# Transpositions, value products and score products issued one by one between the projection matmuls of a two-layer attention trunk, and another order of a layer's first weight splits

## The reference

```python
h = rms_norm(x, norm1_g)
(a_q, a_k, a_v, b_q, b_k, b_v, c_qkv, d_cq, d_ckv, d_kr, gates) = split(h @ w_in)
oa = windowed_gqa(a_q, a_k, a_v, ...)           # 8 heads, band of 128
ob = differential_attention(b_q, b_k, b_v, ...) # 4 heads x 2 maps, full
oc = dilated_attention(c_qkv, ...)              # 3 patterns x 8 heads, softmax over patterns
od = latent_attention(d_cq, d_ckv, d_kr, ...)   # 8 heads, full, two low-rank projections
merged = sum(sigmoid(gate_i) * (o_i @ w_branch[i]) for i, o_i in enumerate((oa, ob, oc, od)))
x = x + merged @ w_o
u = depthwise_conv(rms_norm(x, norm2_g) @ ffn_w_up, ...)
x = x + (silu(g) * up) @ ffn_w_down             # g, up = split(u)
```

## Time and profile before

| | |
|---|---|
| three runs, median (lowest to highest) | 3001.43 us (2998.47 to 3010.02) |
| the profiled execution's own time | 3004.72 us |
| its span, first to last instruction | 3002.9 us |
| PE busy / weight loads busy | 2820.7 / 2267.0 us |
| DVE / ACT busy | 1566.0 / 1179.0 us |
| mean granted TensorE clock | 0.978 of 2.4 GHz |
| matmuls (and as many weight loads) | 13358 |

### The profile page before, as it was taken

One profiled execution on the slowest core, in us unless ns is written; L12 is line 12 of the kernel. 1 busy time (PEld: TensorE's weight loads), 2 busy tenths in 40 slices (PEclk: granted clock), 3 DMA queues, 4 the chain that ended last, 5 costly groups with the idle time before them and its releaser, 6 DMA issues.

```text
span 3002.9 us, 44753 instructions
## 1 busy us (share of the span) xinstructions
PE 2820.7 (94%) x13358; PEld 2267.0 (75%) x13358; DVE 1566.0 (52%) x3238; ACT 1179.0 (39%) x2387; POOL 0.6 (0%) x5
## 2 busy tenths in 40 slices
PE   5999989989989998999979999898899899999998
PEld 4889978666667887888868898776666678788887
DVE  5454476444445445555644544764354454465655
ACT  4444444434433234332434444534444332342432
POOL 0000000000000000000000000000000000000000
PEclk9999999889999999999989999999999999999999
DMA  4212222001112332333332122220111123223332
GB/s 152 72 48 72 78 63 85 12 29 41 45 37 78 94 96 78 99 98 99 99 100 64 44 78 79 67 85 1 36 43 50 31 91 98 92 85 98 95 96 91
DMA packets 141819, 217.62 MB, mean 72 GB/s; under 512 B 14777, under 2 KB 69387, under 8 KB 141195
## 3 DMA queue, kind: packets, MB, share of 16 engines
q1 hardware_dynamic: 132521, 200.62, 21.4%
q10 hardware_dynamic: 9058, 14.06, 1.4%
HBM read 206.20 MB, written 8.45 MB: 71 GB/s over the span
## 4 chain that ended last, share of the span: by engine, by line
PE 81%; DVE 9%; ACT 4%; issue 4%; ACTq 1%; DMA 1%; DVEq 0%; SPq 0%
PE bank L452 21%; PE bank L454 20%; PE bank L453 20%; PE bank L665 7%; PE bank L655 6%; PE bank L503 5%; DVE s_work L1563 1%; DVE s_wl L1139 1%; ACT s_wh L776 1%; ACT s_work L1027 1%; DVE s_work L1294 1%; PE bank L539 1%; ACTq L874 1%; DMA s_raw<-in_w_in 0%; ACT s_work L1019 0%
## 5 line engine op out<-in xcount | busy, mean ns | idle before, releaser
L1139 DVE TENSOR_TENSOR s_wl<-s_raw,s_wh 128x1024 fp32r<-128x1024 f32 (+2 forms) x372 | 453.6, 1220 | 526.5 <-ACT s_wh L776 525.9
L776 ACT ACTIVATE s_wh<-s_raw 128x1024 fp32r<-128x1024 f32 (+2 forms) x372 | 392.2, 1055 | 625.1 <-PE bank L454 591.9
L452 PE MATMUL bank<-s_hTh,s_wh 128*128 128x512 f32 x1216 | 486.2, 400 | 4.5 <-DVE s_work L1231 4.5
L454 PE MATMUL bank<-s_hTh,s_wl 128*128 128x512 f32 x1216 | 476.9, 392 | 0.0
L453 PE MATMUL bank<-s_hTl,s_wh 128*128 128x512 f32 x1216 | 476.7, 392 | 0.0
L452 PE MATMUL bank<-s_wh,s_hTh 128*128 128x512 f32 (+1 forms) x1088 | 475.8, 437 | 0.0
L454 PE MATMUL bank<-s_wh,s_hTl 128*128 128x512 f32 (+1 forms) x1088 | 427.0, 392 | 0.0
L453 PE MATMUL bank<-s_wl,s_hTh 128*128 128x512 f32 (+1 forms) x1088 | 426.7, 392 | 0.0
L1019 ACT ACTIVATE s_work<-s_work,s_stat 128x128 f32<-128x128 f32 (+3 forms) x384 | 214.1, 558 | 369.5 <-DVE s_stat L1588 123.0
L1563 DVE COPY s_work<-bank 128x256 f32<-128x256 f32 (+1 forms) x288 | 105.2, 365 | 394.5 <-ACT s_work L1027 391.9
L503 PE MATMUL bank<-s_consts,s_work 128*128 128x128 f32 (+1 forms) x1560 | 250.0, 281 | 47.3 <-DVE s_gTl L1495 14.3
(11 more groups left out here) (166 smaller groups left out, 3199.6 us busy)
## 6 DMA issues: line engine op xcount, KB each, us to landing
s_raw<-in_w_in SPq DMA_DIRECT2D x168, 512.0 KB, 3.4
s_raw<-in_ffn_w_up SPq DMA_DIRECT2D x176, 256.0 KB, 2.9
s_raw<-in_ffn_w_down SPq DMA_DIRECT2D x44, 512.0 KB, 3.7
s_raw<-in_w_branch SPq DMA_DIRECT2D x32, 512.0 KB, 3.6
s_raw<-in_w_o SPq DMA_DIRECT2D x16, 512.0 KB, 3.6
x_keep<-s_work ACTq DMA_DIRECT2D x2, 2048.0 KB, 7.5
s_raw<-in_w_in SPq DMA_DIRECT2D x16, 256.0 KB, 2.9
s_work<-x_keep ACTq DMA_DIRECT2D x2, 2048.0 KB, 8.2
```

The costliest lines, as they stand in the source:

```text
L452: mm(out, stationary[0], moving[0], start=start, stop=False)
L454: return mm(out, stationary[1], moving[0], start=False, stop=stop)
L776: a(wh[:, k % 3, 0:n], raw[:, s, 0:n], ACT.Copy).then_inc(*hi_split.up(own))
L1139: v.tensor_tensor(wl[:, k % 3, 0:n], raw[:, k % 2, 0:n], wh[:, k % 3, 0:n].bitcast(F32), ALU.subtract).then_inc(*tile_split.up(own))
```

## The change

A piece is now issued in parts. `transposed` yields between any two transpositions, `block` after every single dense matmul (1/6 of a step), and the values yield between any two key pieces. In a unit the transposition now comes right behind the scores (0.1 of the slot, then every 0.1), the values at 0.5 (then every 0.06), and the transposition of an output tile at 0.75 of step 10, 18, ... and no longer at the start of step 11, 19, .... The copies move with them. B's window reaches to four steps before gate1a, which doubles its length, and the norm of B's output follows it. Scores are still issued whole, between two single dense matmuls.

At the start of a layer ScalarE splits tiles 0 and 1 before it squares, and tile 2 after the second chunk of `norm_out`. VectorE splits tile 0 before the norm, tile 1 behind its parameter copy, and tile 2 after the second chunk.

```diff
-    ... B=(START["gate3a"] + 1, START["gate0a"], 32),
+    ... B=(START["gate3a"] + 1, START["gate1a"] - 4, 32),
...
                         for c in range(chunks):
-                            st, mv = operands(b, chunks * i + c, [t[:, c, :] for t in w])
-                            last = split3(PJ[b][:, 0:width], st, mv, i == 0 and c == 0, i == ntiles - 1 and c == chunks - 1)
+                            for st, mv in split3(*operands(b, chunks * i + c, [t[:, c, :] for t in w])):
+                                if n:
+                                    yield START[name] + 4 * i + b + n / (3 * chunks)
+                                n += 1
+                                last = mm(PJ[b][:, 0:width], st, mv, start=i == 0 and n == 1, stop=i == ntiles - 1 and n == 3 * chunks)
...
-            def transposed(dst, sources, at=0):
+            def transposed(dst, sources, done, when, pace, at=0):
 
-                for n, src in enumerate(sources, at):
+                for n, src in enumerate(sources):
+                    if n:
+                        yield when + n * pace
                     k, m = src.shape[0], src.shape[1]
-                    last = nc.tensor.transpose(dst[0:m, n * P:n * P + k], src, ident[0:k, 0:k])
-                return last
+                    last = nc.tensor.transpose(dst[0:m, (at + n) * P:(at + n) * P + k], src, ident[0:k, 0:k])
+                last.then_inc(*done.up())
...
+                yield from transposed(TD, sources, td_ready, when, 1 / 6)
...
+                        yield from transposed(TA, [probs[:, u % 2, P * k:P * k + P] for k in range(lo, hi)], ta_ready,
+                                              at + 0.1 * pace, 0.1 * pace, at=lo)
+                    if 2 <= step < n + 2:
+                        yield at + 0.5 * pace
...
+                        for k, (out, st, mv, start, stop) in enumerate(values_of(u, O1, probsT[:, u % 2, :])):
+                            if k:
+                                yield at + (0.5 + 0.06 * k) * pace
+                            last = mm(out, st, mv, start=start, stop=stop)
...
-            normalise()
-            for _k in range(3):
-                split_next()
+            split_next()
+            normalise()
...
             v.tensor_copy(prm[:, NROW + 88:NROW + 176], src[:, 256:344]).then_inc(*td_dve.up(own))
+            split_next()
...
-            norm_out(ROW["norm1"])
+            norm_out(ROW["norm1"], split_next)
```

More of the change, by code:

```diff
@@ L586, in dense, with turn @@
                     hidden += 2 * size
-            def turn(sources, *ready):
+            def turn(when, sources, *ready):
+                yield when
                 for handle, count in ready:
@@ L603, in head_turns @@
                     for t in range(4):
-                        yield begin + pace * t
                         n += 1
-                        turn(sources_of(t), normed.at(l, n))
+                        yield from turn(begin + pace * t, sources_of(t), normed.at(l, n))
                 def chunks_of(src):
@@ L629, in turns @@
                 for t in range(4):
-                    yield START["gate0a"] + 10 + 1.25 * t
-                    turn([oB[:, t, P * c:P * c + P] for c in range(4)], sublayer_normed.at(l, t + 1))
+                    yield from turn(B_NORM + 9 + 1.25 * t, [oB[:, t, P * c:P * c + P] for c in range(4)], sublayer_normed.at(l, t + 1))
             def attention(name, scores_of, values_of, per_out, begun, keys=all_keys, tile_of=None):
@@ L639, in attention @@
                 for step, at, pace in slots(name):
-                    if tile_of and step >= 11 and (step - 11) % 8 == 0:
-                        yield at
-                        tile = (step - 11) // 8
-                        pe.wait_ge(*o_out.at(l, outs + tile + 1))
-                        pe.wait_ge(*ta_act.at(l, n_att[0]))
-                        pe.wait_ge(*ta_dve.at(l, n_att[0]))
-                        n_att[0] += 1
-                        transposed(TA, tile_of(tile)).then_inc(*ta_ready.up())
                     if step < n:
@@ L656, in attention @@
                         last.then_inc(*s_ready.up())
[L657 to L666 removed]
                     if 1 <= step < n + 1:
[L668 removed]
+                        yield at + 0.1 * pace
                         u = step - 1
@@ L730, in _ @@
             pe.wait_ge(*params_in.at(l, 0))
-            turn([rows[:, n, :] for n in range(3)])
+            together(turn(0, [rows[:, n, :] for n in range(3)]))
             together(dense(), turns(), attentions())
@@ L1003, in attention @@
                 for step, at, pace in slots(name):
-                    if tile_at is not None and step >= 11 and (step - 11) % 8 == 0:
-                        yield at + 0.02 * pace
-                        t = (step - 11) // 8
-                        hi_out(gTh[:, tile_at:tile_at + 4, P * t:P * t + P], att_group(), ta_act)
                     if step < n:
@@ L1027, in attention @@
                         a(probsT[:, u % 2, P * lo:P * mid], src[:, P * lo:P * mid], ACT.Copy).then_inc(*ta_act.up(own))
+                    if tile_at is not None and step >= 10 and (step - 10) % 8 == 0:
+                        yield at + 0.82 * pace
+                        t = (step - 10) // 8
+                        hi_out(gTh[:, tile_at:tile_at + 4, P * t:P * t + P], att_group(), ta_act)
             def attentions():
@@ L1214, in normalise, with norm_out @@
                     v.tensor_scalar(h_sb[:, t, :], x_sb[:, t, :], stat[:, 2, t:t + 1], None, ALU.mult).then_inc(*h_normed.up(own))
-            def norm_out(row):
+            def norm_out(row, after_two=lambda: None):
                 for c in range(DC):
+                    if c == 2:
+                        after_two()
                     n_norm[0] += 1
@@ L1511, in turns @@
                 yield from k_out(END["Bk"] + 6, kT, "bk")
-                begin = START["gate0a"] + 1
+                begin = B_NORM
                 for t in range(4):
@@ L1551, in attention @@
                         biased(step, scores[:, step % 2, :])
-                    if 2 <= step < n + 2 and (step - 2) % per_out == per_out - 1:
-                        yield at + 0.4 * pace
-                        dve.wait_ge(*o_ready.at(l, first + step - 1))
-                        out(step - 2)
                     if 1 <= step < n + 1:
-                        yield at + 0.77 * pace
+                        yield at + 0.58 * pace
                         u = step - 1
@@ L1563, in attention @@
                         v.tensor_copy(probsT[:, u % 2, P * mid:P * hi], src[:, P * mid:P * hi]).then_inc(*ta_dve.up(own))
+                    if tile_at is not None and step >= 10 and (step - 10) % 8 == 0:
+                        yield at + 0.88 * pace
+                        t = (step - 10) // 8
+                        cols = slice(P * t, P * t + P)
+                        lo_out(gTl[:, tile_at:tile_at + 4, cols], gTh[:, tile_at:tile_at + 4, cols], att_group(), ta_dve)
+                    if 2 <= step < n + 2 and (step - 2) % per_out == per_out - 1:
+                        yield at + 0.97 * pace
+                        dve.wait_ge(*o_ready.at(l, first + step - 1))
+                        out(step - 2)
             def attentions():
```

60 lines of the change are left out of this document (29 added, 31 removed).

## The result

| | before | changed |
|---|---|---|
| median of four runs (lowest to highest) | 3004.54 us (2998.47 to 3010.02) | 3068.28 us (3066.43 to 3070.27) |
| span of the profiled execution | 3002.9 us | 3068.5 us |
| mean granted TensorE clock | 0.978 | 0.976 |

The ratio is 1.0214, with an interval of 1.0194 to 1.0234: the change costs 64 us, twice what was forecast. The direction, the largest term (+41) and the start of a layer (-9) came out as forecast; the other terms did not.

A forecast was written before the change was run, and what follows sets the result against it. TensorE was taken to bound the kernel, busy 2820.7 of 3002.9 us. Terms 41 + 5 + 3 - 14 + 6 - 9 = +32 us on 3004.7 (median 3001.4) gave 3034 us; range 2988 to 3070.

The forecast's parts named there:

- The small products, +41: C1 and C2 projections: 376 new places of small products each pay a 0.22 load instead of 0.11, +41 us.
- Other places, +5: Other projections: 982 new places of small products cost between nothing and 0.01 us each, +5 us (0 to 10).
- The start, -9: Start of a layer: earlier splits let TensorE begin sooner, winning 5 us a layer, 4 in layer 0: -9 us.
- Waits in A and B, -14: A's and B's stretches: shorter TensorE waits win 3 us a layer in A, 4 in B: -14 us (0 to -30).
- 0.7 of a slot: A's stretch: dense matmul time between the last transposition and the next needing its copies; before, half a slot to the values.
- The pause, +3: Pause: period 2.6 us a unit, wait moves to the transposition, output tiles cost more; +3 us (-15 to +10).
- TensorE's 2.41 a unit: Pause: TensorE's own work per unit in us; if all waits went, it would give 9 us a layer.
- Turns, +6: Some eight turns a layer that wait for the one before end 0.7 us later: +6 us in all (0 to 11).
- rival 1: Pause, A and B: the waits go and the time falls, to 2979 us with all 65 us won; chance 0.13.
- rival 2: C1 and C2 projections: the long load is hidden, or half as long behind a single product; 2993 us, chance 0.08.
- rival 3: C1q to C2v: the clock falls where small products are spread, 25 to 35 us on top, 3065 us; chance 0.14.

The follow-up runs named there:

- experiment 1: Changed kernel with the six dense matmuls of a step issued in one piece again from C1q to C2v: 3022.75 us, 1.0066 of the kernel before.
- experiment 2: Changed kernel without the reordering of tokens in C1 and C2, so no step in the stationary operand (another output): 3006.42 us, 0.9999 of the kernel before.
- experiment 3: Kernel before without the reordering of tokens in C1 and C2, so no step in the stationary operand (another output): 2987.49 us, ratio 0.9935.
- experiment 6: Kernel before with only the new order of a unit; steps whole, old window of B, old start: 3023.97 us, ratio 1.0059.
- experiment 11: Kernel of experiment 9 plus the new start of a layer and single issue outside C1q to C2v: 2958.32 us, 0.9844 of the kernel before.
- experiment 7: Kernel before with only single issue, at the old places of a unit, old window of B, old start: 3059.2 us, ratio 1.0189.
- experiment 9: Kernel of experiment 6 with ScalarE's copy issued ahead of the next exponential and VectorE's copy earlier: 2959.5 us, 0.985 of the kernel before.
- experiment 8: Kernel before with the new start and B's longer window with its norm behind it, all else old: 2995.78 us, ratio 0.9968.
- experiment 5: Changed kernel with every step's six dense matmuls issued in one piece in all projections: 3032.72 us, 1.0089 of the kernel before.

## Why the prediction was right or wrong

- **The small products, +41:** right in the mechanism. C1q to C2v gave +42.2, and experiments 1, 2 and 3 tie it to the 0.21 load behind a small product. That the size fits to one us has some luck in it: the new order alone takes 4.5 us off this stretch (experiment 6), and against experiment 1 the 366 new places cost 46.7, 0.13 each. In the changed kernel a pair of dense matmul and transposition there starts every 0.46 us (PE), its loads 0.46 apart:

```profile
185.60 0.27 PE L508 MATMUL bank<-s_consts,s_work 128*128 128x128 f32 x1
185.62 0.60 PE L476 MATMUL bank<-s_wh,s_hTl 128*128 128x512 f32 x1
186.06 0.27 PE L508 MATMUL bank<-s_consts,s_work 128*128 128x128 f32 x1
...
185.60 0.31 PEld L476 LDWEIGHTS bank<-s_wh,s_hTl 128*128 128x128 f32 x1
185.85 0.14 PEld L508 LDWEIGHTS bank<-s_consts,s_work 128*128 128x128 f32 x1
186.06 0.31 PEld L476 LDWEIGHTS bank<-s_wh,s_hTh 128*128 128x128 f32 x1
```

  In C0k, without the step, a pair takes 0.34:

```profile
75.36 0.27 PE L508 MATMUL bank<-s_consts,s_work 128*128 128x128 f32 x1
75.39 0.48 PE L476 MATMUL bank<-s_wh,s_hTl 128*128 128x512 f32 x1
75.71 0.27 PE L508 MATMUL bank<-s_consts,s_work 128*128 128x128 f32 x1
76.05 0.27 PE L508 MATMUL bank<-s_consts,s_work 128*128 128x128 f32 x1
```

  The difference is 0.12. The rule of the Trainium skill that the prediction quoted ("TensorE: Matmul & The Clock Gate", section "LDWEIGHTS (loading the stationary operand)") gives 107 ns for both; these runs agree with it where the operand has no step; where it has one the load takes 0.21, and the measurement decides.
- **Other places, +5:** right as far as it can be told. The single pair above costs 0.34 - 0.23 = 0.11 to 0.12, and experiment 11's 0.005 a place gives 982 x 0.005 = 5 us.
- **The start, -9:** right: -8.4.
- **Waits in A and B, -14: the step that failed.** "I take 3 a layer" for A and "4 a layer" for B became -0.2 in Bk and Bv, and +6.2 from gate3a to br1b: +6.0 together, 20 us off.

  In A half of the mechanism was there: single issue alone wins 8.4 us in Bk and Bv (experiment 7). What the prediction left out is what it had itself written down for the pause: in the new order ScalarE's copy stands behind the next unit's exponential. I carried that into the pause's count and not into A's, where I weighed only the place of the values and took "0.7 of a slot" for slack. Order alone costs 12.0 us there (experiment 6), and with the copy moved ahead Bk and Bv take 92.8 and 93.9 (experiment 9).

  In B the wait of the earlier trace rows fell from 7.46 to 4.99 us, 2.5 a layer and not half of it. The rest was taken back by waits that the forecast had not counted: behind the longer window the wait for B's norm grew, from 2.1 us in both layers to 6.9 (4.7 in experiment 8), here layer 0's:

```profile
PE bank L508 <- DVE s_work L1534: 3.5, 1, 3.5
```

  Dense matmuls now wait 1.5 us a layer for VectorE to empty a bank (L476, for L1241). All waits from gate3a to br1b are 11.4 us a layer; before they were 11.5 and 12.1. So nothing was won in waits. The copies have little to do with it: moving them brings this stretch 2.7 us in both layers. Against the whole steps of experiment 5 it is 4 us a layer longer, with a lower clock; the changed kernel and experiment 5, layer 0:

```profile
823.25:1124.84 301.59, 290.18 (x1330) 212.03 (x1328) 137.16 (x257) 94.06 (x167) 0.00 (x0) 0.98 0.22 71
803.10:1100.70 297.60, 285.21 (x1330) 212.57 (x1328) 137.07 (x258) 93.51 (x167) 0.00 (x0) 0.99 0.24 71
```

  Why order, single issue and window together cost 6.2 us there, and each alone -8.6, +2.6 and (with the start) -4.3, stays open.

- **The pause, +3:** the wait and its place were right, and the stretch came out at +9.3, which can't be read as a size. A unit at the full clock takes 2.50 us, near the 2.6 worked out, and the wait stands at the transposition. But the stretch hangs on how long the lower clock lasts. The pause itself, before, in layers 0 and 1:

```profile
547.06:655.73 108.67, 93.28 (x481) 64.94 (x479) 50.63 (x134) 45.44 (x113) 0.00 (x0) 0.85 0.02 6
2038.23:2139.33 101.10, 84.25 (x480) 57.45 (x479) 50.01 (x134) 44.98 (x113) 0.00 (x0) 0.95 0.02 6
```

  In the changed kernel it takes 105.6 and 105.1 us, at 0.87 and 0.88. Of the +9.3, 1.4 are layer 0's and 7.9 layer 1's, where the kernel before had the better clock. With TensorE's order of before the stretch took 171.8 to 184.8 us, so the +3 is neither confirmed nor refuted. What the count did miss is the version in which the waits go. "TensorE's 2.41 a unit" as its floor (0.25 us less for each of 32 units, which is 8 us a layer and not 9) was wrong: with scores, transposition, values in that order a unit is 0.44 + 0.84 + 0.92 = 2.20.
- **Turns, +6:** too small. C0k with C0v, kv with cq, and gate2a to br2b give +15.5 together. In C0k and C0v the rise is 1.2 us a layer, and one wait ahead of a turn makes up 1.1 of it; the turn in the changed kernel, then the same before:

```profile
74.96 0.33 PE L508 MATMUL bank<-s_consts,s_work 128*128 128x128 f32 x1 [1.38 <-DVE s_work L1469]
78.20 0.66 PE L503 MATMUL bank<-s_consts,s_work 128*128 128x128 f32 x4 [0.26 <-DVE s_work L1459]
```

  From kv to br2b the forecast had only turns stretched by single issue; but the new order alone, with steps whole, costs 13.4 us there (experiment 6), and no term had that. From gate2a to br2b the shares of order (+9.6) and single issue (+7.8) don't add up to the +7.8 of both. VectorE is busy for most of gate2a, so each may use up the same slack once; that is only argued, no run parts it.
- **Rivals.** The waits did not go (rival 1): they moved, and those for the copied probabilities did go with the copies placed first. The long load isn't hidden (rival 2: experiments 2 and 3). The clock did not fall from C1q to C2v (rival 3): it is 1.00 with 262 places as with 74, and 0.976 over the run for 0.978. Its price of 3065 lies close to the measured 3068 by accident.

The largest sum lay outside the question I had asked. I asked what the change does to waits that exist; the copies' place behind the exponential decides between +18 us and -41 us for the same order of TensorE (experiments 6 and 9, against the kernel before in their jobs).

## What to carry to other kernels

In these runs a transposition between dense matmuls cost about one weight load, 0.11 us, alone or in a group. Where the dense operand's own load was the longer one (0.21), each place at which small products stand cost the difference once more: keep them in groups there. When the order on one engine is changed, place the operations of the other engines that free its buffers anew; here the copy that frees the bank belonged ahead of an exponential that nobody waited for so soon, and this was worth 2.1%. Before a term of some us is read from one profiled execution, look at the granted clock of its stretch: with the same order the stretch around the pause differed by up to 13 us. A term found in one stretch (a copy queued behind an exponential) has to be carried through every stretch that has the same order.

## What was not expected of the hardware

- Scores with 96 rows in the stationary operand cost less behind values than between transposition and values: 0.92 us from their start to the next transposition (rows of experiment 9), 1.27 less 0.25 idle before; values followed by scores take 0.84, followed by a transposition 0.94. The runs don't say why.
- The granted clock in the pause rose to 0.99 when a unit's period fell to 2.20 us and its wait was gone. With the waits, 0.25 us a unit before and 0.30 in the changed kernel, it lay anywhere between 0.79 (experiment 8) and 0.97 (experiment 6), and differed between layers and executions of one order. Here is the pause in experiment 6, layers 0 and 1, and in experiment 9, layer 0:

```profile
553.87:658.34 104.47, 90.21 (x480) 62.39 (x479) 50.68 (x134) 42.58 (x113) 0.00 (x0) 0.88 0.02 6
2055.06:2152.53 97.47, 82.28 (x481) 56.30 (x479) 50.35 (x134) 42.56 (x113) 0.00 (x0) 0.97 0.02 7
554.59:640.27 85.68, 77.05 (x480) 56.06 (x479) 50.75 (x134) 44.25 (x113) 0.00 (x0) 0.99 0.03 7
```

  The copies' place wins 18.8 us in layer 0 and 11.8 in layer 1. The 7 us between the two are what the clock adds in layer 0, by estimate; no run holds the clock fixed.
